# Conv rows through a scratch laid out by channel: one write and one read per channel tile

## What is computed

```python
def conv_group(u_val, u_gate, conv_w, conv_b, ln_g, ln_b):
    v = u_val * jax.nn.sigmoid(u_gate)                       # GLU
    y = lax.conv_general_dilated(v, conv_w[:, None, :], window_strides=(1,), padding=((CONV_WIDTH - 1, 0),),
        dimension_numbers=("NWC", "WIO", "NWC"), feature_group_count=C_CONV) + conv_b   # depthwise, width 31, causal
    mu = jnp.mean(yf, axis=-1, keepdims=True)
    var = jnp.mean(jnp.square(yf - mu), axis=-1, keepdims=True)
    yf = (yf - mu) * lax.rsqrt(var + LN_EPS) * ln_g + ln_b
    return jax.nn.silu(yf)

u = rms_norm(h, norm_mix_g) @ w_in                           # (B, L, 2576)
c_val, c_gate, q, k, v, g, gate_lr = jnp.split(u, split_idx, axis=-1)
h = h + jnp.concatenate([conv_group(...), gla_group(...)], axis=-1) @ w_out
h = h + swiglu(rms_norm(h, norm_ffn_g), w_ffn_gate, w_ffn_up, w_ffn_down)
```

## Time and profile before

| | |
|---|---|
| median of 3 runs | 1591.3 us |
| the profiled execution, its own time | 1589.89 us |
| its span (core 3, the slowest; the cores have 1568.5 to 1588.3) | 1588.3 us |
| PE (matmul) busy | 1451.3 us, 91% |
| DVE / ACT / POOL busy | 792.8 / 546.1 / 290.1 us |
| chain that ended last: PE / DMA | 74% / 14% |
| transfers `rep<-vsc` | 32 by SP, 96 by POOL, 134.0 KB each |
| transfers `vsc<-vT` | 32 by SP, 136.0 KB each |
| transfers `wring<-wsc` | 303 by SP, 512.0 KB, 4.9 us to landing (median) |

### The profile page before, as it was taken

One profiled execution on the slowest core, in us unless ns is written; L12 is line 12 of the kernel. 1 busy time (PEld: TensorE's weight loads), 2 busy tenths in 40 slices (PEclk: granted clock), 3 DMA queues, 4 the chain that ended last, 5 costly groups with the idle time before them and its releaser, 6 DMA issues.

```text
span 1588.3 us, 26641 instructions; the slowest of 8 cores (1568.5 to 1588.3 us)
## 1 busy us (share of the span) xinstructions
PE 1451.3 (91%) x8194; PEld 686.6 (43%) x8194; DVE 792.8 (50%) x1758; ACT 546.1 (34%) x964; POOL 290.1 (18%) x411
## 2 busy tenths in 40 slices
PE   2947699998999989999999989999899989999996
PEld 1433344444444444444444434444444434444442
DVE  4556338524565156643484345743375443843423
ACT  3445253415424244224533035222442245311111
POOL 1131042123500133002400124002230033000000
PEclk9978899999999999999999989999999999999998
DMA  9968688799988994399845996469934896456541
GB/s 189 210 172 192 140 185 179 175 218 236 248 207 214 225 277 156 134 216 197 258 139 166 219 188 217 126 201 195 264 122 154 215 176 216 143 158 188 199 159 66
DMA packets 138298, 299.43 MB, mean 189 GB/s; under 512 B 50336, under 2 KB 71200, under 8 KB 138160
## 3 DMA queue, kind: packets, MB, share of 16 engines
q1 hardware_dynamic: 75152, 203.21, 41.5%
q0 software_dynamic: 24480, 85.08, 27.7%
q10 hardware_dynamic: 38528, 9.44, 4.8%
HBM read 280.18 MB, written 46.40 MB: 206 GB/s over the span
## 4 chain that ended last, share of the span: by engine, by line
PE 74%; DMA 14%; issue 3%; DVE 3%; ACT 2%; SPq 1%; POOL 1%; DVEq 0%; ACTq 0%; POOLq 0%
PE ps L671 53%; PE ps L1285 16%; DMA wring<-wsc 8%; DMA vsc<-vT 2%; DMA wring<-wpack 2%; SPq L820 1%; PE ps L650 1%; DMA rep<-vsc 1%; PE ps L766 1%; DMA out<-h 1%; DMA gfin<-norm_final_g 1%; PE ps L874 1%; PE ps L1194 0%; PE ps L1162 0%; PE ps L1167 0%
## 5 line engine op out<-in xcount | busy, mean ns | idle before, releaser
L671 PE MATMUL ps<-x2T,wring 128*128 128x512 bf16 x2816 | 646.3, 384 | 36.9 <-DMA wring<-wsc 24.3
L671 PEld LDWEIGHTS ps<-x2T,wring 128*128 128x128 bf16 x2816 | 274.6, 99 | 369.7 <-issue 59.3
L1285 PE MATMUL ps<-wring,actT 128*128 128x512 bf16 x1408 | 310.6, 379 | 0.8 <-DMA wring<-wpack 0.5
L1269 DVE SCALAR_TENSOR_TENSOR ftmp<-ftmp,ps 128x512 f32<-128x512 f32 x176 | 120.5, 685 | 257.7 <-ACT ftmp L1268 239.4
L1268 ACT ACTIVATE ftmp<-ps 128x512 f32<-128x512 f32 x176 | 104.9, 596 | 346.0 <-PE ps L671 328.4
L1285 PEld LDWEIGHTS ps<-wring,actT 128*128 128x128 bf16 x1408 | 136.8, 98 | 167.9 <-issue 7.5
L671 PE MATMUL ps<-xT,wring 128*128 128x512 bf16 x736 | 168.2, 384 | 6.1 <-ACT xT L655 3.4
L1271 DVE SCALAR_TENSOR_TENSOR actT<-ftmp,ps 128x512 bf16<-128x512 f32 x176 | 120.0, 685 | 68.7 <-PE ps L671 64.2
L820 POOL DMA_DIRECT2D rep<-vsc x96 | 53.9, 569 | 444.6 <-PE ps L1285 204.9
L671 PE MATMUL ps<-wring,yT 128*128 128x512 bf16 x512 | 121.5, 387 | 10.5 <-DMA yT<-rep 5.6
L671 PE MATMUL ps<-wring,xT 128*128 128x512 bf16 x512 | 118.5, 381 | 0.3 <-ACT actT L769 0.3
(11 more groups left out here) (178 smaller groups left out, 1191.2 us busy)
## 6 DMA issues: line engine op xcount, KB each, us to landing
wring<-wsc SPq DMA_DIRECT2D x303, 512.0 KB, 4.9
wring<-wpack POOLq DMA_DIRECT2D x79, 512.0 KB, 8.9
wsc<-wring SPq DMA_DIRECT2D x48, 512.0 KB, 7.3
h<-xin POOLq DMA_DIRECT2D x28, 512.0 KB, 11.6
out<-h POOLq DMA_DIRECT2D x28, 512.0 KB, 6.5
rep<-vsc POOLq DMA_DIRECT2D x96, 134.0 KB, 10.4
vsc<-vT SPq DMA_DIRECT2D x32, 136.0 KB
rep<-vsc SPq DMA_DIRECT2D x32, 134.0 KB, 8.5
```

The source lines that it names most:

```text
L671: ins = e.matmul(pt_ap, lhsT=lhs(kc), rhs=rhs(kc), start=(kc == 0), stop=(kc == KC - 1))
L1269: P.add("dve", lambda e: e.scalar_tensor_tensor(out=th[:], in0=th[:], scalar=1.0, in1=pg[:], op0=ALU.add, op1=ALU.mult), R=[Bpg, Bth], W=[ ...
L1285: ins = e.matmul(ps[t][:], lhsT=actT[:, j, t * 128:(t + 1) * 128], rhs=wd3[:, j - j0, :], start=(j == 0), stop=(j == NJ - 1))
```

## The change

The scratch `vsc` gets a layout of four channel tiles x two token phases x 16 rows, where one row is eight channels of 272 elements after each other. A channel tile is written with one transfer of 256 pieces of 544 bytes (the two phases of a channel are no longer neighbours) and read with one transfer into all 128 partitions: four shifts x 32 rows of 2172 elements, 4344 bytes each. The source of the read is an access pattern whose first dimension is the four shifts with a step of one element. So a block has 4 writes and 4 reads in place of 4 and 16. Each read waits for its own tile's write alone. The writes go to the queue that has the reads: SP in the first two blocks, POOL in the other six. The channels of a tile are grouped in another way, so the host arranges the convolution weights, the vectors and the first 512 rows of `w_out` to match. The pitch of `rep` grows from 268 to 272; room for it comes from `stn` (four slots in place of eight, used twice in the first block) and from three constants in one tile.

```diff
-    vsc = nc.dram_tensor("vsc", [2, 16, 4, 8, 2 * (16 + HT)], BF16, kind="Internal").ap()
+    vsc = nc.dram_tensor("vsc", [2, 4, 2, 16, 8 * (16 + HT)], BF16, kind="Internal").ap()
...
-        rep = sb("rep", [128, 4, 8, 12 + HT], BF16)
+        rep = sb("rep", [128, 4, 8, 16 + HT], BF16)
...
-        stn = sb("stn", [128, 2 * NT, 6])
+        stn = sb("stn", [128, NT, 6])
...
-        gb = sb("gb", [128, 2])
-        cvec = sb("cvec", [128, 3, 8])
-        gng = sb("gng", [128, 1])
+        small = sb("small", [128, 27])
+        cvec, gb, gng = small[:, 0:24].rearrange("p (k n) -> p k n", k=3), small[:, 24:26], small[:, 26:27]
...
-            Brep = [[Buf(f"rep{c}_{i}") for i in range(8)] for c in range(4)]
-            Bvsc = [[[Buf(f"vsc{k}_{i}_{c}") for c in range(2)] for i in range(2)] for k in range(2)]
+            Brep = [[Buf(f"rep{c}")] for c in range(4)]
+            Bvsc = [[Buf(f"vsc{k}_{c}") for c in range(4)] for k in range(2)]
...
-                            xni["m"] = norm(h[2][3], Bh[2][3], gmix, NT, [Bpre])
+                            xni["m"] = norm(h[2][3], Bh[2][3], gmix, 0, [Bpre])
...
-                        cs, Bv = slice(c - 1, c + 1), Bvsc[bi % 2][i]
-                        src = vsc[bi % 2]
+                        eng = "pool" if bi > 1 else "sp"
+                        src, Bv, n = vsc[bi % 2], Bvsc[bi % 2], 8 * (16 + HT) - 4
                         for k in (c - 1, c):
-                            P.add("sp", lambda e, k=k: e.dma_start(out=src[:, k].rearrange("q g n -> g q n"),
-                                                                   in_=vT[:, k].rearrange("p a n -> p (a n)")),
-                                  R=[BvT[k], Bhist[k]], W=[Bv[k - c + 1]], dkey=f"vs{bi % 2}_{k}")
-                        rows = src[:, cs].rearrange("q c g n -> q (c g) n")
-                        for s_ in range(8):
-                            n0 = (s_ % 2) * (16 + HT) + 4 - s_ // 2
-                            P.add("pool" if bi > 1 else "sp", lambda e, s_=s_, n0=n0: e.dma_start(
-                                out=rep[s_ * 16:(s_ + 1) * 16, cs].rearrange("p c g n -> p (c g) n"), in_=rows[:, :, n0:n0 + 12 + HT]),
-                                R=Bv, A=[Bycv[c - 1], Bycv[c], Bysq[c - 1], Bysq[c]],
-                                W=[Brep[c - 1][s_], Brep[c][s_]], dkey=f"{'prep' if bi > 1 else 'rep'}{i}_{s_}")
+                            P.add(eng, lambda e, k=k: e.dma_start(out=src[k].rearrange("a q (g n) -> (q g) a n", g=8), in_=vT[:, k]),
+                                  R=[BvT[k], Bhist[k]], W=[Bv[k]], dkey=f"{eng}vs{bi % 2}_{k}")
+                        for k in (c - 1, c):
+                            rows = src[k].rearrange("a q n -> (a q) n")[:, 1:1 + n]
+                            rows = bass.AP(tensor=rows.tensor, offset=rows.offset, ap=[[1, 4], [8 * (16 + HT), 32], [1, n]])
+                            P.add(eng, lambda e, k=k, rows=rows: e.dma_start(
+                                out=rep[:, k].rearrange("p g n -> p (g n)")[:, 0:n], in_=rows),
+                                R=[Bv[k]], A=[Bycv[k], Bysq[k]], W=Brep[k], dkey=f"{eng}rep{k}")
...
-                        transp(norm(h[hs][t], Bh[hs][t], gffn, NT + t), x2T[:, t], Bx2T[t], False)
+                        transp(norm(h[hs][t], Bh[hs][t], gffn, t), x2T[:, t], Bx2T[t], False)
...
+    w_out = np.concatenate([regroup(w_out[:CC]), w_out[CC:]], axis=0)
```

More of the change, by code:

```diff
@@ L377, in build @@
             Bxn = [Buf(f"xn{i}") for i in range(3)]
-            Bst = [Buf(f"st{i}") for i in range(2 * NT)]
+            Bst = [Buf(f"st{i}") for i in range(NT)]
             Bstb = [[Buf(f"stb{i}_{t}") for t in range(NT)] for i in range(2)]
@@ L1425, in cols, with regroup @@
         return w[k0 * 128:(k0 + nk) * 128, c0:c0 + n].reshape(nk, 128, n).transpose(1, 0, 2).reshape(128, nk * n)
+    def regroup(v):
+        return v.reshape(4, 16, 2, 4, -1).transpose(0, 2, 3, 1, 4).reshape(v.shape)
     w_in, w_out = f("w_in")[0], f("w_out")[0]
+    w_out = np.concatenate([regroup(w_out[:CC]), w_out[CC:]], axis=0)
     w_fg, w_fu, w_fd = f("w_ffn_gate")[0], f("w_ffn_up")[0], f("w_ffn_down")[0]
@@ L1442, in make_in_maps @@
     wg2[:, 0:16, :] = f("gla_w_gate2")[0]
-    cw = np.zeros((33, 4, 8, 16), np.float32)
-    cw[1:32] = f("conv_w")[0][::-1].reshape(31, 4, 8, 16)
+    cw = np.zeros((33, 4, 16, 8), np.float32)
+    cw[1:32] = f("conv_w")[0][::-1].reshape(31, 4, 16, 8)
     conv_w4 = np.zeros((4, 2, 16, 4, 8, 4, 2), np.float32)
@@ L1449, in make_in_maps @@
                 for a in range(2):
-                    conv_w4[i, ph, :, :, :, w, a] = cw[8 * w + 2 * i + 1 - ph + a].transpose(2, 0, 1)
+                    conv_w4[3 - i, ph, :, :, :, w, a] = cw[8 * w + 2 * i + 1 - ph + a].transpose(1, 0, 2)
     conv_w4 = conv_w4.reshape(128, 4, 8, 4, 2)
-    vecs = np.stack([np.repeat(f(k)[0].reshape(8, 64).T, 2, axis=0) for k in ("conv_b", "conv_ln_g", "conv_ln_b")], axis=1)
+    vecs = np.stack([np.repeat(regroup(f(k)[0]).reshape(8, 64).T, 2, axis=0) for k in ("conv_b", "conv_ln_g", "conv_ln_b")], axis=1)
     common = {
```

## The result

The changed kernel takes 1655.3 us (median of four runs, 1652.5 to 1662.5) beside 1591.3 for the kernel before on the same chip (median of three): a ratio of 1.0405, 95% interval 1.0360 to 1.0449. In some executions, whatever the kernel, the cores of one die show a lower granted clock and take longer; these are left out of all times and ratios here, and where one was profiled (the kernel with its writes back on SP) the rows are of a core on the other die. The forecast was 1566, range 1548 to 1588. The profiled execution took 1656.39 us; its slowest core is core 4 with a span of 1654.8, the others have 1629.2 to 1648.4. Every core is slower than the slowest one of before.

A forecast was written before the change was run, and what follows sets the result against it. PE, 91% busy, was held up by late blocks' small-piece reads and a start wait. Core 3: 1588.3 - 24 - 7 + 3 = 1560; core 6: 1568; slowest put at 1564, plus 1.6 gives 1566 us, range 1548 to 1588.

The forecast's parts named there:

- What bounds the kernel: Late blocks: small-piece reads use up the DMA engines, PE waits for weights; 24 us of 29.6 gained on core 3.
- the start: First block's convolution wait: gain of 7 us with reads on four engines, 11.8 us over 16.
- Price of the reads and of the writes: Per block: new reads 118 engine-us, 152 less; writes at most 68 more; 84 to 152 engine-us set free.
- upper bound of 68: Per block, new writes take 68 engine-us more if old writes cost nothing, priced from a read piece at 66 ns.
- No relief: Rival, late-block reads: two queues sharing HBM, not piece length, set their price; 1583 to 1592 us, chance 0.08.
- the last rival: "Slower", six POOL blocks: four reads on the same four engines, convolution copies late by 11 us a block; 1625, chance 0.05.
- Costs: Third and fourth blocks: weight loads behind waiting writes and reads on POOL; 0 to 20 us, 3 taken.
- the bad end of the range that was given: First block, reads on four engines: the last read ends at 107, a loss of 8 us.
- the middle: First block, reads on four engines: the last read ends at 93, a gain of 7 us.

The follow-up runs named there:

- the exchanged read: Changed kernel with the read source's two outer dimensions exchanged, 32 rows outermost and four shifts inside, weights arranged to match: 1564.1 us, ratio 0.9807 to the kernel before.

## Why the prediction was wrong, step by step

**What bounds the kernel: right.** The small pieces in the late blocks were what held PE up. With the read exchanged, core 3's span behind 300 us is

```profile
300.00:1560.90 1260.90, 1225.58 (x6798) 577.25 (x6796) 640.30 (x1372) 427.54 (x752) 196.30 (x259) 0.99 0.69 196
```

and PE stands 35.3 us where it stood 61.5. These 26.2 us and 1.2 of busy time make the 27.4 us that core 3 gained. The late blocks gave rather more, since core 3 came to 300 us with less done (PE busy 220.2 us, 224.5 before; the start, below). The forecast had 24 for this.

**Price of the reads and of the writes: right for the reads, writes within the bound.** In the late block of the exchanged read, the queue of POOL from 913 to 940 us (packets, MB, share of 16 engines):

```profile
q0 software_dynamic: 707, 2.65, 31.5%
```

31.5% of 16 x 27 us is 136 engine-us for 2.65 MB, of which the four reads are 2.22: 19.5 GB/s for an engine, where 18.8 was taken from `out<-h` and the old reads had 8.0. From 903 to 916 the same queue carried two of the new writes and nothing else:

```profile
q0 software_dynamic: 96, 0.28, 10.6%
```

10.6% of 16 x 13 us is 22 engine-us for two, 44 a block, against an upper bound of 68 that came from the price of a read piece. "No relief" falls.

**The step that failed: the four engines stopped at the start.** The prediction asked what happens if a read is dealt out over four engines, priced it for the start only, and let the sum for the six POOL blocks use 16 engines. For those blocks it left four engines to the last rival, at 0.05, and there it looked at one consequence, the convolution waiting for its copies past 951, and dismissed it because an engine moves 20 GB/s. On that point the dismissal holds, though not for its reason: of the 9.5 us that PE waits for `rep<-vsc` in the whole span, 7.3 are in the first block. An engine moved 10 to 26 GB/s (68 GB/s at a share of 0.41, 60 at 0.28, 104 at 0.25), which is on both sides of the 12 at which the rival was to decide; and POOL's reads did not all run on the same four engines, as the 0.51 of two at once shows. But the price falls elsewhere. A transfer over few engines makes late what is queued with it: the next write on POOL's queue (14.0 us in the median, 9.4 with the exchanged read), the tiles from `wpack` (15.3 in the third block, 11.2 before), and on POOL all that stands behind a read that waits for its write. It did not reach everything that the theory had named: the rows of `h` by POOL landed in 9.7 us in the median (11.6 before), SP's loads from `wsc` in 4.9 as before. The "Costs" paragraph had this chain, with 8.77 us as the longest landing wait and 3 us in the sum; 8.77 came from the old reads and writes, and the wait became 14.2 in the third block and 25.47 in the last one, where the write had been issued right behind a read:

```profile
1340.33 0.73 POOL L818 DMA_DIRECT2D rep<-vsc  x1 [3.58 <-ACT mtmp L786]
1341.05 0.73 POOL L813 DMA_DIRECT2D vsc<-vT  x1
...
1369.13 0.73 POOL L818 DMA_DIRECT2D rep<-vsc  x1 [25.47 <-DMA vsc<-vT]
```

So instead of 3 us of costs there were 39.5 us of waits for `wpack` (35 more than before), 15.3 for `mtmp` (12 more), which POOL computes later, and a lowered clock (0.67 in the stretch from 365), and the 24 us of `wsc` were not given back: 22.3 are left on core 4.

The Trainium skill's rule in "DMA: Bandwidth & Descriptors", section "Why a DMA increments its semaphore by 16 and not by 1", fits the runs: a slowest dimension of 4 was 91 us slower than one of 32 over the same bytes, and the share of 0.25 is the four engines that it gives. The Trainium skill has in this section a rotating choice of engines for POOL's transfers; the 0.51 of two reads at once agrees, but in these runs it did not protect POOL's blocks, which carried five sixths of the loss. No row here names the engines.

**The start: wrong in both kernels.** In the changed kernel the second half of the first convolution began at 107.24 us (99.25 before), after 7.28 us of waiting for its read: a loss of 8, the bad end of the range that was given, not the middle. With 16 engines that wait is gone, but the 11.8 us forecast for this case came on one core only: the first convolution ends 12.2 us sooner on core 0 (93.41 for 105.56), 3.4 sooner in the median of the cores, and 2.7 later on core 3. PE's timeline of core 3 in the exchanged kernel:

```profile
96.51 1.06 PE L1097 MATMUL ps<-x2T,k_tm 128*64 128x128 bf16 x16 [7.41 <-DVE actT L1152]
...
99.35 5.96 PE L874 MATMUL ps<-rep,wcv 128*32 128x256 bf16 x128 [0.94 <-DVE S L1112]
```

The convolution ends at 105.31 there and at 102.58 before. The wait moved ahead of it, and ACT's timeline on the same core says to what:

```profile
86.69 0.60 ACT L1151 ACTIVATE actT<-ps 128x512 f32<-128x512 f32 x1 [1.09 <-PE ps L673]
93.84 1.06 ACT L631 ACTIVATE actT<-h 128x1024 bf16<-128x1024 f32 x1 [6.55 <-DMA h<-xin]
...
94.89 0.58 ACT L1151 ACTIVATE actT<-ps 128x512 f32<-128x512 f32 x1
```

Before, all four gate activations (L1151) stood ahead of the norm of the next rows of `h`:

```profile
82.35 0.60 ACT L1151 ACTIVATE actT<-ps 128x512 f32<-128x512 f32 x1 [1.13 <-PE ps L671]
84.41 1.06 ACT L629 ACTIVATE actT<-h 128x1024 bf16<-128x1024 f32 x1 [1.46 <-DMA h<-xin]
```

In the new order the norm stands ahead of the fourth one and waits for a load, and attention waits with it. The changed kernel has the same order on ACT and 10.8 us of this wait. The prediction went through the order of SP and POOL, not through that of ACT.

**The number.** 1566 is close to the 1564 of the read over 16 engines, though not by the terms of the sum, so this is in part luck: more from the late blocks (27 on core 3 behind 300 us, in place of 24 less 3), less from the start (3.4 in the median of the cores, in place of 7). As a forecast for the change as it was made it missed by 89 us, because one access pattern decides it.

## What to carry to other kernels

Before pricing a transfer by its bytes and piece length, read the outermost dimension of its source: four there gave a quarter of the engines, and naming the same pieces with the 32 rows first was worth 91 us. When a resource is confined like that, its price isn't only its own landing: list what else uses it, and price the queue behind the one who waits for that. And when a change lets a scheduler move instructions, look at its order on every engine on the path of the wait that is to go, ACT here, since the next wait in the chain limits the gain.

## What the runs showed of the hardware

- A read whose source has 4 as its outermost dimension kept four of 16 engines busy: share 0.25, 26 GB/s for an engine, even with four such reads queued on SP. Two of POOL's at once kept eight (0.51).
- On POOL's queue a write landed with the read issued ahead of it: 19.9 us behind reads of 20.0, 4.7 ahead of any read.
- A DMA share of 0.28 with PE at a stop: a mean over 16 engines hides that the few which matter are full. Before the change the same symptom came with a share near 1.
- Issuing the single read over four shifts costs POOL 0.72 us, the same read with 32 rows first 0.56, a write 0.73.
- The new writes were cheap on the engines, 22 engine-us for two. What was expensive beside them, from 903 to 916 us, were ACT's transposes, 0.52 MB for 55.7% of 16 x 13 us, 4.5 GB/s for an engine:

```profile
q10 hardware_dynamic: 2082, 0.52, 55.7%
```
